# Fourteen of the input-projection tiles of a hybrid decoder step in seven Strassen pairs, with GpSimd making the weight sums

## What is computed

```python
h = rms_norm(x, p['pre_g'])                       # (tokens, 1024)
proj = jnp.einsum('bsd,de->bse', h, p['w_in'])    # 1024 -> 3360 columns, in twelve parts
(c_b, c_c, c_x, c_gate, r_sh, r_gate, q_down, ckv_raw, kr_raw, mla_gate, mem_q, mem_gate) = _split(proj, IN_SPLITS)
conv_out = short_conv(c_b, c_c, c_x, ...)          # gated convolution
rwkv_out = rwkv7_mix(r_sh, ...)                    # token shift, decay, state recurrence
mla_out  = latent attention over q_down, ckv_raw, kr_raw
mem_out  = cross attention with mem_q over 256 memory tokens
x = x + rms_norm(concat(gated outputs) @ p['w_out'], p['post_g'])
```

## Time and profile before

| | |
|---|---|
| median of 3 runs | 3639.87 us (3639.13 to 3640.68) |
| profiled execution | span 3638.2 us from its first to its last instruction; no time of its own stands beside it |
| what lies around the span, by the median | 1.7 us |
| PE busy | 3534.1 us, 97% |
| DVE, ACT, POOL busy | 1695.0, 1387.6 and 163.9 us |
| mean granted TensorE clock | 0.994 |

### The profile page before, as it was taken

One profiled execution on the slowest core, in us unless ns is written; L12 is line 12 of the kernel. 1 busy time (PEld: TensorE's weight loads), 2 busy tenths in 40 slices (PEclk: granted clock), 3 DMA queues, 4 the chain that ended last, 5 costly groups with the idle time before them and its releaser, 6 DMA issues.

```text
span 3638.2 us, 74822 instructions
## 1 busy us (share of the span) xinstructions
PE 3534.1 (97%) x30920; PEld 2615.3 (72%) x30920; DVE 1695.0 (47%) x4364; ACT 1387.6 (38%) x3767; POOL 163.9 (5%) x284
## 2 busy tenths in 40 slices
PE   7999999999999999999989999999999999999998
PEld 5768686776768777687567676868767687776864
DVE  2535454454545535445326354554535454353553
ACT  2333434243343433534433333343433434335343
POOL 1000000000000000000000000000000000000000
PEclk9999999999999999999999999999999999999999
DMA  5343343424324143232342524334153241532411
GB/s 177 100 144 107 132 129 111 138 72 162 93 101 147 50 165 91 94 123 67 112 140 84 171 84 154 107 112 137 59 182 96 99 128 48 177 95 79 134 55 66
DMA packets 316645, 411.42 MB, mean 113 GB/s; under 512 B 26501, under 2 KB 276307, under 8 KB 316307
## 3 DMA queue, kind: packets, MB, share of 16 engines
q1 hardware_dynamic: 294771, 360.95, 30.8%
q0 software_dynamic: 11648, 41.95, 3.3%
q10 hardware_dynamic: 9888, 3.74, 0.4%
HBM read 384.81 MB, written 21.80 MB: 112 GB/s over the span
## 4 chain that ended last, share of the span: by engine, by line
PE 89%; ACT 5%; DVE 2%; issue 2%; ACTq 1%; DVEq 0%; DMA 0%; SPq 0%; POOL 0%; POOLq 0%
PE bank L722 82%; PE bank L726 8%; ACT hT L2155 1%; ACT Q L2315 1%; ACTq L2294 1%; ACT L2295 0%; ACT PT L2431 0%; ACT qr L2314 0%; ACT Sm L2388 0%; DVEq L1401 0%; ACT Q L2313 0%; DVE bon L1531 0%; ACT Bp L2336 0%; ACT T L2293 0%; DVE ml L1706 0%
## 5 line engine op out<-in xcount | busy, mean ns | idle before, releaser
L722 PE MATMUL bank<-hT,win 128*128 128x256 f32 (+3 forms) x7168 | 1608.2, 379 | 4.5 <-ACT hT L2155 4.5
L722 PEld LDWEIGHTS bank<-hT,win 128*128 128x128 f32 (+1 forms) x7168 | 1260.2, 187 | 222.7 <-issue 40.7
L722 PE MATMUL bank<-kv,Q 96*128 96x512 f32 (+3 forms) x640 | 276.4, 529 | 0.2
L726 PEld LDWEIGHTS bank<-cst,Sm 128*128 128x128 f32 x1344 | 157.6, 140 | 146.6 <-issue 69.2
L1706 DVE TENSOR_REDUCE ml<-bank 128x1 f32<-128x512 f32 (+3 forms) x320 | 195.5, 611 | 142.7 <-PE bank L722 131.9
L726 PE MATMUL bank<-cst,Sm 128*128 128x128 f32 x1344 | 210.5, 278 | 26.3 <-ACT Sm L2388 17.9
L2388 ACT ACTIVATE Sm<-bank,ml 128x512 f32<-128x512 f32 (+3 forms) x320 | 199.8, 625 | 74.4 <-DVE ml L1711 68.6
L722 PE MATMUL bank<-wout,mix 128*128 128x512 f32 x480 | 219.6, 604 | 6.9 <-ACT hT L2155 6.6
L722 PEld LDWEIGHTS bank<-wout,mix 128*128 128x128 f32 x480 | 89.3, 192 | 114.4 <-issue 113.4
L2177 ACT ACTIVATE mix<-bank 128x256 f32<-128x256 f32 x128 | 49.2, 384 | 318.3 <-PE bank L722 318.3
L2284 ACT ACTIVATE mix<-bank 128x512 f32<-128x512 f32 (+1 forms) x68 | 39.6, 596 | 252.0 <-PE bank L722 252.0
(11 more groups left out here) (483 smaller groups left out, 5673.9 us busy)
## 6 DMA issues: line engine op xcount, KB each, us to landing
win<-in_w_in SPq DMA_DIRECT2D x176, 1024.0 KB, 5.3
wout<-in_w_out SPq DMA_DIRECT2D x60, 512.0 KB, 7.6
out_xres<-xin SPq DMA_DIRECT2D x16, 1024.0 KB
xin<-in_x_prompt SPq DMA_DIRECT2D x15, 1024.0 KB
xin<-out_xres SPq DMA_DIRECT2D x15, 1024.0 KB
win<-in_w_in SPq DMA_DIRECT2D x16, 896.0 KB, 4.8
PT<-in_w_out SPq DMA_DIRECT2D x28, 512.0 KB, 3.6
XX<-in_w_out SPq DMA_DIRECT2D x28, 512.0 KB, 4.1
```

The source lines that it names most:

```text
L722: return pe.matmul(out, lhsT, rhs, start=start, stop=stop, skip_group_check=True)
L726: return pe.transpose(out, in_, ident[0:w, 0:w])
```

## The change

In blocks 1 to 7 of both layers, seven pairs of tiles (1+2, 3+4, 5+6, 9+10, 11+12, 13+14, 15+16: all groups before tile 17 that are 256 wide) are computed as a 2 x 2 product of halves: two halves of the columns, two halves of the 1024 rows, two halves of the 256 tokens. Strassen's form needs seven half products of 4 parts by 128 tokens in place of eight. With A the weights and H the tokens, the sums it needs are made as follows.

- Token sums, once a block, by DVE (`token_sums`, at the end of the block before, ahead of `residual`): four operations of 128x512, into `wout`. The loads of `wout` therefore move from before group 4 to before group 11.
- Weight sums, for each pair, by POOL (`weight_sums`): four operations of 128x512; the first one overwrites a quarter of the slot. The sums of pair 0 are made at the end of the block before, those of pairs 1 and 2 before the 16-column copies, those of pairs 3 to 6 after them.
- Recombination, for each pair: ACT copies the first product out of its bank (`copy_first`), and DVE does five operations, two of 128x256 and three of 128x128 (`take_pair`), in place of ACT's two copies of 128x256. Pairs 5 and 6 are taken by DVE after `s_rt`.

```diff
+            def pair(B, i):
+                t = PAIRS[i]
...
+                n = B.fp * NPAIR + i
+                product(X, 0, A[0][0], H[0][0])
+                product(X, 1, A[0][1], H[1][0])
+                if i == 0:
+                    pe.wait_ge(s_tc.h, s_tc.at(B.fp, 1))
+                pe.wait_ge(s_ws.h, 4 * n + 2)
+                product(X, 2, s[:, 0], tsum[:, 1]).then_inc(s_px.h, 1)
+                decode(B.unit, t)
+                product(Y, 3, A[1][1], tsum[:, 3])
+                product(Y, 0, A[1][0], tsum[:, 0])
+                pe.wait_ge(s_ws.h, 4 * n + 3)
+                product(Y, 1, s[:, 1], tsum[:, 2])
+                pe.wait_ge(s_ws.h, 4 * n + 4)
+                product(Y, 2, s[:, 2], H[1][1]).then_inc(s_pj.h, 2)
+                decode(B.unit, t + 1)
...
+            def weight_sums(B, i):
...
+                pool.wait_ge(s_wi[g % 2].h, s_wi[g % 2].at(B.ip, loads_of_slot(g)))
...
+                pool.tensor_tensor(A[1][0], A[1][0], A[1][1], ADD).then_inc(s_ws.h, 1)
+                pool.drain()
+                pool.tensor_tensor(s[:, 0], A[1][0], A[0][0], SUB).then_inc(s_ws.h, 1)
+                pool.drain()
+                pool.tensor_tensor(s[:, 1], A[1][1], s[:, 0], SUB).then_inc(s_ws.h, 1)
+                pool.tensor_tensor(s[:, 2], A[0][1], s[:, 0], SUB).then_inc(s_ws.h, 1)
...
+            def take_pair(B, i, dst):
...
+                v.wait_ge(s_p1.h, s_p1.at(B.fp, i + 1))
+                v.tensor_tensor(dst[:, 0, :].rearrange("p (a t) -> p a t", a=2), X[:, 1:3, :],
+                                first[i % 2].unsqueeze(1).broadcast_to([P, 2, P]), ADD)
+                drain()
+                v.wait_ge(s_pj.h, s_pj.at(B.ip, t + 2))
+                v.tensor_tensor(partial, Y[:, 0:2, :], dst[:, 0, P:T].unsqueeze(1).broadcast_to([P, 2, P]), ADD)
+                drain()
+                v.tensor_tensor(dst[:, 0, P:T], Y[:, 2, :], partial[:, 0, :], ADD)
+                v.tensor_tensor(dst[:, 1, 0:P], Y[:, 3, :], partial[:, 1, :], ADD)
+                v.tensor_tensor(dst[:, 1, P:T], Y[:, 0, :], partial[:, 1, :], ADD).then_inc(s_pp.h, 1)
+                drain()
```

More of the change, by code:

```diff
@@ L142, in __init__ @@
         self.bank = 0 if self.last else 4
+        self.fast = bool(block)
+        self.fp = l * (NB - 1) + block - 1 if self.fast else None
 class Sig:
@@ L785, in tile, with product @@
                     last.then_inc(s_pj.h, 1)
+            def pair(B, i):
+                t = PAIRS[i]
+                g = TILES[t][0]
+                w, x, s = win[:, g % 2], hT, wsum[:, (B.fp * NPAIR + i) % 2]
+                halfK = KD // 2
+                X, Y = tile_bank(t), tile_bank(t + 1)
+                def product(bank, q, weights, tokens):
+                    for k in range(halfK):
+                        last = mm(PP[bank][:, q * P:(q + 1) * P], weights[:, k, :], tokens[:, k, :], k == 0, k == halfK - 1)
+                    return last
+                A = [[w[:, a * halfK:(a + 1) * halfK, f * P:(f + 1) * P] for a in range(2)] for f in range(2)]
+                H = [[x[:, a * halfK:(a + 1) * halfK, j * P:(j + 1) * P] for j in range(2)] for a in range(2)]
+                pe.wait_ge(s_wi[g % 2].h, s_wi[g % 2].at(B.ip, loads_of_slot(g)))
+                if i == 1:
+                    pe.wait_ge(s_pa.h, s_pa.at(B.ip, 1))
+                elif i in (2, 3, 5):
+                    pe.wait_ge(s_pp.h, s_pp.at(B.fp, {2: 1, 3: 3, 5: 4}[i]))
+                elif i == 4:
+                    pe.wait_ge(s_pa.h, s_pa.at(B.ip, 9))
+                elif i == 6:
+                    pe.wait_ge(s_rw.h, s_rw.at(B.it, 1))
+                n = B.fp * NPAIR + i
[13 more added lines that the diff above has]
+                decode(B.unit, t + 1)
             def project(B):
@@ L790, in project @@
                     pe.wait_ge(s_sbk.h, s_sbk.at(B.l, B.block))
+                if B.fast:
+                    tile(B, 0)
+                    decode(B.unit, 0)
+                    for i in range(3):
+                        pair(B, i)
+                    tile(B, 7)
+                    decode(B.unit, 7)
+                    tile(B, 8)
+                    lora(B)
+                    decode(B.unit, 8)
+                    pair(B, 3)
+                    key_norms(B)
+                    pair(B, 4)
+                    latent_norms(B)
+                    pair(B, 5)
+                    pair(B, 6)
+                    return
                 for t in range(17):
@@ L2176, in take_tile, with copy_first @@
                         act.activation(sproj[0:f, t, :], PP[bank][0:f, T:T + NS], ACT.Copy)
-                    act.activation(o, PP[bank][0:o.shape[0], 0:T], ACT.Copy).then_inc(s_pa.h, 1)
+                    tiles = {7: 7, 17: 9}.get(t, 1) if B.fast else 1
+                    act.activation(o, PP[bank][0:o.shape[0], 0:T], ACT.Copy).then_inc(s_pa.h, tiles)
+                def copy_first(B, i):
+                    act.wait_ge(s_px.h, s_px.at(B.fp, i + 1))
+                    if i >= 2:
+                        act.wait_ge(s_pp.h, s_pp.at(B.fp, i - 1))
+                    act.activation(first[i % 2], PP[tile_bank(PAIRS[i])][:, 0:P], ACT.Copy).then_inc(s_p1.h, 1)
                 def begin(B):
```

93 lines of the change are left out of this document (80 added, 13 removed).

## The result

The changed kernel takes 3711.99 us (median of 4 runs, 3709.28 to 3714.14); the kernel before, run beside it on the same chip, 3639.5 us. The ratio is 1.0204, with a 95% interval of 1.0192 to 1.0217. So it is slower, as forecast, and within the range, but by 72 us and not by 28.

What follows compares the result with a forecast made beforehand. PE, busy 97% of the span, was taken as the bound. Per block 4.8 - 1.6 - 1.2 - 0.9 - 3.1 = -2.0 us, times 14 a loss of 28 us: 3668 us (+0.8%), range 3580 to 3720.

Steps and rivals of the forecast that it cites:

- PE's saving: In paired projections, 56 narrow matmuls at 0.111 us save 0.69 us per pair, 4.8 per block, 3.9 net of 0.9 waiting.
- Rival 4: On PE, weight loads are not hidden at 128 columns: 5.5 us more per pair, 4176 us in all; chance 0.03.
- The price of a sum: On POOL, one weight sum of 128x512 takes 1.2 us; four with two drains take 5.1 us per pair.
- rival 3: POOL becomes the bound with sums of 1.6 us or more, 6.7 us per pair: 3717 us and up; chance 0.13.
- My own case: POOL's sums of 1.0 to 1.4 us hold up DVE: 3668 us, own range 3632 to 3698; chance 0.50.
- DVE and POOL hold each other: During POOL's sums, each DVE operation on two SBUF inputs waits up to 1.06 us.
- the 3.1: Before the bonus, pair 6's sums hold DVE's ten operations three of four times: 3.1 us on top of 0.9.
- The middle term: Between slot 11 and `s_sq` 2, three holds by pair 5's sums stretch 2.6 us to 4.7: PE waits 1.2.
- The step that failed first: The block's sum, ending at the bonus: PE's waits outweigh its saving by 2.0 us, 28 us over 14 blocks.
- The step that failed second: In POOL's queue, tile 8's copies stand behind two sets of sums, 10 us that fit in: no cost.
- the forecast part of the loss: From tile 0 to the bonus in 14 blocks: a loss of 28 us.

Runs made afterwards that it cites:

- e2: The changed kernel without any of POOL's weight sums, three of seven products taking plain weights: 3584.95 us, ratio 0.9854.
- e1: The changed kernel with the sample root ahead of the sums of pair 0 in POOL's queue in blocks 0: 3698.93 us, ratio 1.0168.
- e3: The changed kernel with three products on plain weights and POOL adding constants in place of the sums, nobody waiting for them: 3710.95 us, ratio 1.02.
- e7: e3 with the order of e1 and POOL's additions half as wide, 128x256: 3616.7 us, ratio 0.9944.
- e5: e1 with ten pairs of unread 256-column identity matmuls on PE before the wait for the bonus: 3672.16 us, ratio 1.0105.
- f2: e1's order, with the sums of all seven pairs made in block 1, written to DRAM and loaded in later blocks: 3604.14 us, ratio 0.9915.

## Why the prediction was right in its mechanism and short in its size

**PE's saving: right.** 0.112 us per narrow matmul; 3.84 us net in block 4 without sums (3.76 on average), against 3.9. Rival 4 is out.

**The price of a sum: right, a little low.** 1.26 to 1.27 us alone, 1.34 to 1.46 on average beside DVE, for 1.2 forecast. The estimate of 1.3 us, worked out from the figure of the Trainium skill (GPSIMD Engine Reference, 3.1), was the better number. POOL kept up: PE waited for it inside a pair only once in the 98 (1.15 us, block 4 of layer 1). So rival 3 did not come, though its time (3717) is the nearest of all. The range reaches up to 3720 only to take in the near end of rival 3; that it holds the measured 3712 is luck. My own case ended at 3698.

**DVE and POOL hold each other: right, place by place.** Between e2 and e1 (both without the order's cost) PE's slip in block 4, counted from tile 0 (858.26 and 881.33), grows by 1.60 us at slot 3 (starts at 872.83 and 897.50), by 1.19 at `latent_norms` (912.77 and 938.63) and by 3.23 at the bonus (927.01 and 956.10). The forecasts were 1.6, 1.2 and 3.1. How the 3.1 is made up was partly wrong: not three long two-input operations, but one of them (0.85 us) and the two `TENSOR_SCALAR` (1.86), with 0.5 for DVE's backlog (its first operation starts 6.07 us behind `latent_norms` in e1 and 5.54 in e2). The middle term does not follow from what the prediction writes down either: three full holds of 1.06 us on 2.6 make 5.8 us, not 4.7, so the 1.2 is right without its working being right, and in the changed kernel itself that wait shows in 4 of 14 blocks (in the others the wait ahead of the bonus is longer instead). e3 shows that the sums do it by running, and e7 that their length sets it.

**The step that failed first** is the one that stopped the sum at the bonus: "Sum per block: 4.8 - 1.6 - 1.2 - 0.9 - 3.1 = -2.0, a loss; times 14 is 28 us". It priced the wait and put what follows the wait at nothing. In block 4 PE idled for 3.84 us, and the granted clock was 0.50 over the next 5 us, a stretch of short dependent matmuls, and 0.94 over the 5 us after them. That cost 29.8 us over 14 blocks, 2.1 each. e5 showed that it is the clock and not the lateness of DVE. The Trainium skill (TensorE: Matmul & The Clock Gate, Part 1, What's actually happening) says that the clock falls to 1.2 GHz once the engine has been idle; the granted 0.50 at 962.07 agrees. I had looked up that page for its weight loads and not asked of each forecast wait what it does to the clock.

**The step that failed second** is "The order of POOL's queue puts the copies for tile 8 behind two sets of sums [...] nothing". The copies were the right thing to ask about there, but I did not ask the same of the fourth place where sums were put, ahead of the sample root in blocks 0: 13.9 us, shown by e1. Of the 7.0 us in each block 0, 5.4 are the wait, and most of the rest is the clock behind it, the first failed step once more. All sums in that queue first wait for a load, and everything behind them inherits that wait.

30.6 + 29.8 + 13.9 = 74.3, less 1.5 elsewhere, is the 72.8 us of the spans. What stays open is the condition under which a wait of about 2.2 us lowers the clock, and the column "other", up to 2.9 us, whose places were not looked into.

## What to carry to other kernels

When a forecast says that TensorE will wait for a few microseconds, price what follows the wait at the lower clock too, or give the engine something to do in it; here it was 2.1 us a block behind waits of 3.8 to 4.7 us, and over the whole kernel as much as the forecast part of the loss (29.8 against 30.6 us). Work handed to GpSimd is not free because GpSimd is idle: place it by what DVE does at that time, and look at each instruction that stands behind it in its queue. What depends on the weights alone is made once and loaded again, if the DMA queues have room.

## What was not expected of the hardware

- Two `TENSOR_SCALAR` operations of 128x256 on DVE with a single SBUF tensor as input, together 0.62 us, took 2.16 us beside POOL's fills, which read nothing, while a two-input addition beside them stayed at 0.69.
- Twenty idle-time matmuls per block, whose results nobody reads, bought 26.8 us (by the medians) of a kernel whose PE is busy 95% of the span.
- The four DMAs of one pair in f2, 1.75 MB in all, landed 4.0 to 7.2 us after their issues (medians), while the tiles before were computed; PE waited for them 0.7 us in the whole run.
